# Both softmax heads scaled by GpSimd instead of one by VectorE and one by GpSimd

## The reference

```python
s = jnp.einsum('bhqd,bhrkd->bhqrk', qb, kb).astype(jnp.float32) * scale + bias
s = jnp.where(col_in[:, None, :], s, -jnp.inf)
s_ctx = jnp.einsum('bhqd,bhcd->bhqc', qb, kc).astype(jnp.float32) * scale
p = jax.nn.softmax(jnp.concatenate([s.reshape(...), s_ctx], axis=-1), axis=-1)
p_lat = p[..., :kr * GRID_W].reshape(B, NA_HEADS, GRID_W, kr, GRID_W)
return jnp.einsum('bhqrk,bhrkd->bhqd', p_lat, vb) + jnp.einsum('bhqc,bhcd->bhqd', p[..., kr * GRID_W:], vc)
```

## Time and profile before

| | us |
|---|---|
| median of 3 runs | 3042.29 (3042.14 to 3043.86) |
| the profiled execution | 3042.29 |
| its span, first to last instruction | 3040.0 |
| TensorE busy | 2929.7 (96%) |
| VectorE busy | 1563.7 (51%) |
| ScalarE busy | 1041.9 (34%) |
| GpSimd busy | 432.4 (14%) |
| mean granted clock of TensorE | 0.983 of full |

### The profile page before, as it was taken

One profiled execution on the slowest core, in us unless ns is written; L12 is line 12 of the kernel. 1 busy time (PEld: TensorE's weight loads), 2 busy tenths in 40 slices (PEclk: granted clock), 3 DMA queues, 4 the chain that ended last, 5 costly groups with the idle time before them and its releaser, 6 DMA issues. The chain is left out here.

```text
span 3040.0 us, 38095 instructions
## 1 busy us (share of the span) xinstructions
PE 2929.7 (96%) x15799; PEld 2395.6 (79%) x15799; DVE 1563.7 (51%) x1943; ACT 1041.9 (34%) x1265; POOL 432.4 (14%) x351
## 2 busy tenths in 40 slices
PE   5899999999999999999999999999799999999998
PEld 3787787878888888888888877777677888888886
DVE  5668567264444444444463144545436454445445
ACT  5586775141112211111142344444323222222123
POOL 3121230200000000000033433333210000000002
PEclk8999999999999999999999999999899999999999
DMA  7443334222212111212222433332511111111111
GB/s 283 127 131 100 115 98 147 65 77 77 70 56 70 63 56 63 70 49 63 70 77 91 139 79 92 91 81 68 184 49 42 56 42 49 49 49 43 48 49 56
DMA packets 259846, 249.18 MB, mean 82 GB/s; under 512 B 45707, under 2 KB 230619, under 8 KB 253531
## 3 DMA queue, kind: packets, MB, share of 16 engines
q1 hardware_dynamic: 247835, 192.62, 21.0%
q0 software_dynamic: 11776, 54.13, 5.6%
q10 hardware_dynamic: 64, 0.01, 0.0%
HBM read 212.45 MB, written 31.26 MB: 80 GB/s over the span
## 5 line engine op out<-in xcount | busy, mean ns | idle before, releaser
L704 PE MATMUL ps<-zH,wH 128*128 128x512 f32 (+1 forms) x2048 | 751.4, 367 | 5.7 <-ACTq L1090 4.3
L704 PE MATMUL ps<-zL,wH 128*128 128x512 f32 (+1 forms) x2048 | 749.1, 366 | 0.0
L704 PE MATMUL ps<-zH,wL 128*128 128x512 f32 (+1 forms) x2048 | 748.3, 365 | 0.0
L704 PEld LDWEIGHTS ps<-zH,wH 128*128 128x128 f32 x2048 | 386.8, 189 | 85.9 <-issue 13.8
L704 PEld LDWEIGHTS ps<-zL,wH 128*128 128x128 f32 x2048 | 386.9, 189 | 62.4
L704 PEld LDWEIGHTS ps<-zH,wL 128*128 128x128 f32 x2048 | 386.8, 189 | 62.5
L2233 DVE SCALAR_TENSOR_TENSOR res<-ps,mod,res 128x1024 f32<-128x1024 f32 x240 | 236.7, 1014 | 186.4 <-PE ps L704 175.3
L714 DVE SCALAR_TENSOR_TENSOR V<-ps,vec,V 128x1023 f32<-128x1023 f32 x126 | 128.1, 1016 | 369.7 <-ACT V L2092 366.7
L2065 ACT ACTIVATE wH<-wraw 128x1024 fp32r<-128x1024 f32 x130 | 134.6, 1050 | 388.6 <-PE ps L704 388.6
L704 PE MATMUL ps<-hH,wH 128*128 128x512 f32 (+1 forms) x700 | 260.3, 372 | 0.3 <-DVE res L2233 0.3
L704 PE MATMUL ps<-hL,wH 128*128 128x512 f32 (+1 forms) x700 | 258.3, 369 | 0.0
(11 more groups left out here) (318 smaller groups left out, 4966.1 us busy)
## 6 DMA issues: line engine op xcount, KB each, us to landing
wraw<-in_ffn_w_up_dram SPq DMA_DIRECT2D x88, 512.0 KB, 3.9
modw<-in_mod_w_dram POOLq DMA_DIRECT2D x40, 1024.0 KB, 5.2
wraw<-in_ffn_w_down_dram SPq DMA_DIRECT2D x44, 512.0 KB, 3.3
wraw<-in_na_w_in_dram SPq DMA_DIRECT2D x32, 512.0 KB, 4.0
bias<-scratch_bias SPq DMA_DIRECT2D x512, 32.0 KB, 1.8
modring<-in_mod_w_dram SPq DMA_DIRECT2D x8, 1024.0 KB, 14.3
wraw<-in_rg_w_in_dram SPq DMA_DIRECT2D x16, 512.0 KB, 4.8
v<-scratch_v SPq DMA_DIRECT2D x128, 64.0 KB, 2.0
```

Source lines behind the costliest of these rows:

```text
L704: last = nc.tensor.matmul(ps[:, slot * SLOT + c:slot * SLOT + c + n], w(k), r(k)[:, c:c + n], start=(k == 0 and i == 0), stop=(k == K - 1 ...
```

## The change

GpSimd now scales both heads, head 0 first, and VectorE's scaling instruction is gone, with its wait for `recip`. The two semaphores `scaled[0]` and `scaled[1]` become one, `scaled`, that counts two per turn; TensorE waits for `2 * g + 1` before head 0's transposes and for `2 * g + 2` before head 1's. Nothing else is changed; three lines fewer move the later line numbers up by one to three.

```diff
-    s_done, s_biased, exp_done, recip = [sem("na_" + n) for n in ("s_done", "s_biased", "exp_done", "recip")]
-    scaled = [sem("na_scaled0"), sem("na_scaled1")]
+    s_done, s_biased, exp_done, recip, scaled = [sem("na_" + n) for n in ("s_done", "s_biased", "exp_done", "recip", "scaled")]
...
     def gpsimd(gp):
         def scale(g):
             gp.wait_ge(recip, g + 1)
-            x = m.S[:, g % 2, 1, 0:WIDTH[g % 2]]
-            nc.gpsimd.tensor_scalar(x, x, m.rowstat[:, g % 2, 5:6], None, ALU.mult).then_inc(scaled[1], 1)
+            for hd in range(2):
+                x = m.S[:, g % 2, hd, 0:WIDTH[g % 2]]
+                nc.gpsimd.tensor_scalar(x, x, m.rowstat[:, g % 2, 4 + hd:5 + hd], None, ALU.mult).then_inc(scaled, 1)
...
         def turn(g):
             for hd in range(2):
-                pe.wait_ge(scaled[hd], g + 1)
+                pe.wait_ge(scaled, 2 * g + hd + 1)
...
         def inverse(g):
             dve.wait_ge(exp_done, 2 * g + 2)
             nc.vector.reciprocal(m.rowstat[:, g % 2, 4:6], m.rowstat[:, g % 2, 2:4]).then_inc(recip, 1)
-            dve.wait_ge(recip, g + 1)
-            x = m.S[:, g % 2, 0, 0:WIDTH[g % 2]]
-            nc.vector.tensor_scalar(x, x, m.rowstat[:, g % 2, 4:5], None, ALU.mult).then_inc(scaled[0], 1)
```

## The result

The changed kernel takes 3068.89 us in the median (3067.81 to 3069.94, 4 runs) against 3042.26: a ratio of 1.0086, 95% interval 1.0070 to 1.0101. It is 26.6 us slower; 29.9 were forecast. Its profiled execution was shorter than the timed ones, 3065.21 us with a span of 3063.4.

What follows compares the result with a forecast made beforehand. Bound: TensorE, busy 96%; the question was latency within a turn, from reciprocal to transposes. Pairs 14.3 us plus end 8.8 made 23.1; clock falls 6.8 gave 29.9 on 3042.29, forecast 3072 us, range 3062 to 3086.

Steps and rivals of the forecast that it cites:

- the give-back of the end: Last turns: SyncE's bias DMAs keep up with slower turns, so 4.9 us of waiting over 7.6 us are regained.
- The couple: GpSimd's two scalings of one turn, back to back: 3.76 us at 640 wide, 3.60 us at 608.
- it = 5: Turn of each pair of heads, scalings behind a weight block: last two transposes late by 1.57 us.
- it = 2: Turn of each pair behind the other weight block: late by 0.56 us, part covered by an existing wait.
- it = 7: Turn of each pair where GpSimd starts right behind the reciprocal: head 1's loads late by 0.26 us.
- The end: Turns 55 to 63, without fill, each waiting on GpSimd: nine times 1.52 us, 13.7, less 4.9 regained, 8.8 us.
- VectorE's relief: 64 scalings of 0.55 us, 35 us of work, leave VectorE; nothing on the path waits for them, gain nothing.
- The clock falls in four of six turns it = 5: TensorE idle 2.03 us there; clock falls for 3.4 us, 1.7 us lost each, 6.8 us in all; chance 0.55.
- The clock holds: Rival: TensorE's clock does not fall in the pairs, so 23.1 us remain, 3065 us; chance 0.25.
- The long couple: Rival: GpSimd's extra 0.36 us after idle time stays, 4.12 us for two scalings, 5.4 us more; chance 0.14.
- the paid relief: Rival: TensorE really waits for VectorE, so removing its scaling pays; 3039 us given; chance of faster 0.03.
- the hidden scalings: Rival: GpSimd's 202.9 us of idle time hide the new scalings, 3042 us; chance of no change 0.03.

Runs made afterwards that it cites:

- the mix: Kernel before, but both heads' scalings on VectorE from turn 55 on and the weight blocks one turn later in GpSimd's list: 3044.35 us, ratio 1.0001.
- the pairs-only kernel: Kernel before, but both heads scaled on GpSimd in turns 0 to 54, turns 55 to 63 as before: 3060.74 us, ratio 1.0054.

## Why the prediction was right

Direction and place were right, and the delays of the pairs' turns to 0.1 us each. The sum came out 3.3 us above the measured difference of 26.6; that it came so near is in part luck, since two errors of it point in opposite directions (the clock's falls counted too high, the give-back of the end too).

- **The couple takes 3.76 and 3.60 us.** Right: 3.75 and 3.59. The long form belonged to VectorE's scaling beside it; the run with head 0 unscaled shows it apart. The Trainium skill's rule of the shared port pair ("SBUF — State Buffer", section "SBUF: two separate sides") says that the second of the two engines is blocked fully. The measurement agrees in direction: GpSimd lost 0.35 us to an instruction of 0.55 us that had started 0.06 us before. A full block to its end would be 0.49 us, an estimate by that rule; the runs show less.
- **it = 5 late by 1.57, it = 2 by 0.56, it = 7 by 0.26, the others covered.** Measured 1.51, 0.50 and 0.24, and below 0.1 in each other turn. Together with those small ones six pairs cost 14.2 us (14.3 forecast). The tight case, it = 1 with 0.44 us to spare, was indeed covered.
- **The end costs 13.7 less 4.9, 8.8 us.** Measured 8.35, with the same loop and the same give-back. But the give-back of 4.9 us took in 2.7 us that were the fall of the clock behind the bias wait. Of the five profiles with that wait three had the fall and two didn't. Against executions without it the end costs 11 us, and the 64 turns 25.3 instead of 22.6. I had taken the 12.53 us of the last two turns as a property of the kernel.
- **VectorE's relief gains nothing.** Right: leaving the scaling out gains nothing measurable, doubling it loses nothing.
- **The clock falls in four of six turns it = 5, 6.8 us.** This is the step that was mis-sized. The size of one was right (1.5 to 1.6 us measured, 1.7 estimated), and so was the idle time of the weight loads (2.2 us measured, of which 0.17 also stood before, 2.03 forecast); the count was not: 0, 0, 1 and 2 in four profiles, so 0 to 3.1 us. The sign "the granted clock below 1.0 within the pairs" was missing in two of the four. In the end stretch no fall came before turn 63, as counted.
- **The sum.** The turns give 22.6 us where 23.1 were forecast, the falls 0 to 3.1. The measured 26.6 us lie above even their largest sum. In the profile the whole span grew by 23.4 us: the turns by 22.56, from a start 1.18 us earlier, and 2.0 us behind turn 63. These 2.0 us aren't the change's: the stretch behind turn 63 is 0.65 to 2.45 us longer than in the first profile of before in all eleven others, also with head 0 unscaled (0.65), both heads on VectorE (2.1) and the mix (1.4). It goes loosely with the clock: TensorE has 34 to 46 us at 1.2 GHz in that stretch, the first profile of before 35.2 and the changed kernel's 46.3. Together with the 2.7 us of the fall near the end, which not every execution of before has, this can make up what is missing; for the timed runs, of which there are no profiles, that is argued, not shown.
- **The rivals.** "The clock holds", 3065, is what two of four profiled executions did; forecast and rival are one kernel in different executions. The long couple, the paid relief and the hidden scalings are out.

## What to carry to other kernels

An engine that is idle 86% of the time can still be the wrong place for an instruction: look at when its input arrives and when its output is wanted, turn by turn, not at its load. In a list that runs in order, what stands directly ahead of the new instruction counts most; moving the two weight blocks of each pair by one turn took away more than half of this loss without changing any work. Where a change leaves the matmuls idle for some 1.7 us in front of dense work, as here, put 1.5 us a time for the clock into the far end of the range, not in full into the forecast; and look for such a fall in the profile of before too, since a stall with a fall behind it can cost more there than in the next execution (here 2.7 us more).

## What the runs showed of the hardware that I hadn't expected

- GpSimd's scaling is 0.35 us longer when VectorE's SBUF-to-SBUF scaling starts 0.06 us before it (2.24 against 1.88 us at 640 wide), while VectorE's bias instruction, which reads PSUM and starts some 0.4 us after it, doesn't lengthen it (1.89 us at 640 wide in turns of the changed kernel where it starts so). Whether the source or the later start makes that difference isn't shown. Its time is 0.08 us more for 32 more elements a partition, 2.5 ns an element; VectorE needs 0.55 us for all 640.
- The same instructions with the same gaps lost the clock in 0, 1 or 2 of six places in different executions. With the matmuls' idle time stretched from 1.7 to 3.6 us it was six of six, in one profile.
- The times of one kernel spread by up to 12 us (the pairs-only kernel, 3052.6 to 3065.1), and its slower executions had the lower mean granted clock (0.980 against 0.985).
